# Delta rule heads prepared in two alternating pairs of PSUM banks, in a kernel whose order is written as a plan

## The reference

```python
def even_layer(h, ...):
    p = rms_norm(h, norm_g) @ w_in                       # 2048 x 9232
    qkv_a, z_a, b_a, a_a, glu_b, z_b, q_m, z_m = split(p)
    qkv = silu(causal_depthwise_conv(qkv_a, conv_qkv))   # 4 taps, 3 x 1024 channels
    q, k, v = heads(qkv)                                 # 8 heads of 128
    q = l2_norm(q) * 128 ** -0.5; k = l2_norm(k)
    o = gated_delta_rule(q, k, v, beta, g)               # chunked; needs (I + A)^-1 of each block
    o_a = rms_norm(o, dn_norm_g) * silu(z_a)
    c = causal_depthwise_conv(glu(glu_b), dw_w)          # 31 taps, 1024 channels
    o_b = silu(layer_norm(c)) * silu(z_b)
    o_m = memory_attend(q_m, z_m, ...)
    return concat([o_a, o_b, o_m]) @ w_out
def odd_layer(h, ...):                                   # stick-breaking attention, 16 heads, and memory_attend
```

## Time and profile before

| | |
|---|---|
| median of 3 runs | 1391.09 us (1390.8 to 1392.14) |
| profiled execution | 1390.43 us, of which the span of the core 1388.7 us |
| TensorE busy | 1360.9 us (98%) |
| VectorE busy | 885.6 us (64%) |
| ScalarE busy | 752.8 us (54%) |
| GpSimd busy | 110.5 us (8%) |
| granted TensorE clock, mean | 0.993 |

### The profile page before, as it was taken

The page is one execution under the profiler, slowest core; times in us unless marked ns, Lnnn a source line. Parts: engine busy times, 40 slices in busy tenths (PEclk is TensorE's granted clock), DMA queues, the critical chain, the costliest instruction groups (busy, mean ns, idle before and its releaser), DMA issues.

```text
span 1388.7 us, 17340 instructions
## 1 busy us (share of the span) xinstructions
PE 1360.9 (98%) x6459; PEld 1130.3 (81%) x6459; DVE 885.6 (64%) x1327; ACT 752.8 (54%) x1163; POOL 110.5 (8%) x112
## 2 busy tenths in 40 slices
PE   6999998999989999999999999999999999999998
PEld 5888877888878887888888888888888888888887
DVE  4547698787787898774566544564655645556563
ACT  4545543455524565666444555755756757665341
POOL 1001201010300100000000120020020110000000
PEclk9999999999999999999999999999999999999999
DMA  8565445555554575465365655464564564653652
GB/s 268 194 200 167 154 130 161 150 165 158 146 175 136 186 270 188 130 218 176 123 192 164 212 172 181 140 201 163 177 201 141 177 187 149 191 174 121 195 185 76
DMA packets 134205, 239.27 MB, mean 172 GB/s; under 512 B 13888, under 2 KB 19433, under 8 KB 134121
## 3 DMA queue, kind: packets, MB, share of 16 engines
q1 hardware_dynamic: 131945, 233.96, 53.1%
q10 hardware_dynamic: 2176, 4.19, 0.9%
HBM read 234.32 MB, written 3.80 MB: 171 GB/s over the span
## 4 chain that ended last, share of the span: by engine, by line
PE 93%; DVE 3%; issue 1%; SPq 1%; ACT 1%; DMA 0%; DVEq 0%; ACTq 0%
PE job L1581 27%; PE job L1583 27%; PE job L1582 27%; PE mixer L1601 4%; DVE wlo L1218 1%; PE mixer L1810 1%; PE mixer L1830 1%; PE mixer L1702 1%; DVE reg L1292 1%; PE mixer L1848 1%; PE mixer L1716 0%; PE mixer L1861 0%; PE mixer L1714 0%; DMA raw<-in_ev_w_in_dram 0%; SPq L708 0%
## 5 line engine op out<-in xcount | busy, mean ns | idle before, releaser
L1581 PE MATMUL job<-whi,xhi 128*128 128x512 f32 x1728 | 695.2, 402 | 0.0
L1218 DVE TENSOR_TENSOR wlo<-raw,whi 128x1024 fp32r<-128x1024 f32 x432 | 529.4, 1243 | 239.3 <-ACT whi L890 236.6
L1583 PE MATMUL job<-whi,xlo 128*128 128x512 f32 x1728 | 676.8, 392 | 0.0
L1582 PE MATMUL job<-wlo,xhi 128*128 128x512 f32 x1728 | 675.5, 391 | 0.0
L890 ACT ACTIVATE whi<-raw 128x1024 fp32r<-128x1024 f32 x432 | 445.4, 1056 | 142.3 <-PE job L1583 133.6
L1583 PEld LDWEIGHTS job<-whi,xlo 128*128 128x128 f32 x1728 | 325.7, 189 | 70.9
L1582 PEld LDWEIGHTS job<-wlo,xhi 128*128 128x128 f32 x1728 | 326.9, 189 | 63.2
L1581 PEld LDWEIGHTS job<-whi,xhi 128*128 128x128 f32 x1728 | 326.4, 189 | 63.3 <-issue 0.4
L1442 DVE SCALAR_TENSOR_TENSOR cvr<-cvr,vt 128x255 f32<-128x255 f32 (+14 forms) x240 | 103.5, 491 | 0.0
L917 ACT ACTIVATE proj<-job,rstd 128x512 f32<-128x512 f32 x80 | 50.5, 686 | 50.4 <-PE job L1583 43.9
L1234 DVE TENSOR_TENSOR hid<-hid,job 128x512 f32<-128x512 f32 x48 | 30.8, 683 | 50.6 <-PE job L1583 50.6
(11 more groups left out here) (257 smaller groups left out, 882.9 us busy)
## 6 DMA issues: line engine op xcount, KB each, us to landing
raw<-in_od_w_in_dram SPq DMA_DIRECT2D x160, 512.0 KB, 4.5
raw<-in_ev_w_in_dram SPq DMA_DIRECT2D x144, 512.0 KB, 4.0
raw<-in_ev_w_out_dram SPq DMA_DIRECT2D x48, 512.0 KB, 4.6
raw<-in_od_w_out_dram SPq DMA_DIRECT2D x48, 512.0 KB, 4.7
raw<-in_w_mem_kv_dram SPq DMA_DIRECT2D x32, 512.0 KB, 4.3
hid<-in_x_dram SPq DMA_DIRECT2D x4, 512.0 KB, 7.9
reg<-in_mem_dram ACTq DMA_DIRECT2D x4, 512.0 KB, 6.2
hid<-in_x_dram ACTq DMA_DIRECT2D x4, 512.0 KB, 7.7
```

Of the source, the lines that this page charges most:

```text
L1218: vec.tensor_tensor(wlo[:, c % RING, :, :], raw[:, c % RAWS, :, :], whi[:, c % RING, :, :].bitcast(F32), ALU.subtract).then_inc(s_lo, 1)
L1581: mm(out_, xh, hi, start=first, stop=False)
L1582: mm(out_, xh, lo, start=False, stop=False)
L1583: return mm(out_, xl, hi, start=False, stop=last)
```

## The change

Before, every head was transposed into `mixer0` and `mixer1` and turned back through `mixer2`. Now an even head has `mixer0` and `mixer1` and an odd one `mixer2` and `mixer3`, and each is turned back through the second bank of its own pair (`mixer1` or `mixer3`). The outputs `d7(0)` to `d7(3)` go by turns through `mixer2` and `mixer3` (before: `mixer2`).

In the plan a head takes 3.1 chunks (before 3.5), and `dnB(h - 1)` is placed right behind the next head's `dnT` and `dnC`. Steps that follow in the same stream move with it, those of the convolution only in part. No instruction is added or removed.

```diff
-DN_STEP = 3.5
+DN_STEP = 3.1
...
         for h in range(h0, h0 + 4):
-            s += [(("dnT", h), .2), (("dnC", h), 1.2), (("dnS", h), .9), (("dnU", h), DN_STEP - (2.1 if h > h0 else 1.7))]
-            s += [(("dnB", h - 1), .1)] if h > h0 else []
-        s += [("wait", 1), (("dnB", h0 + 3), 1), (("dnV", g), 2), (("dnR", g), 2.5)]
+            s += [(("dnT", h), .2), (("dnC", h), .6)] + ([(("dnB", h - 1), .6)] if h > h0 else [("wait", .6)])
+            s += [(("dnS", h), .9), (("dnU", h), DN_STEP - 2.3)]
+        s += [("wait", .6), (("dnB", h0 + 3), 1), (("dnV", g), 2), (("dnR", g), 2.5)]
...
             if step == "d7":
-                return [1 if i in (5, 7) else 2]
+                return [2 + i % 2 if i < 4 else 1 if i in (5, 7) else 2]
+            if step in ("dnT", "dnB"):
+                return [0, 1, 2, 3][2 * (i % 2) + (step == "dnB"):2 * (i % 2) + 2]
...
-        def dn_source(c):
+        def dn_source(h, c):
 
-            return (M[0][:, S:2 * S], M[0][:, 0:S], M[1][:, 0:S])[c]
+            m = M[2 * (h % 2):2 * (h % 2) + 2]
+            return (m[0][:, S:2 * S], m[0][:, 0:S], m[1][:, 0:S])[c]
```

More of the change, by code:

```diff
@@ L570, in banks @@
             if step == "d7":
-                return [1 if i in (5, 7) else 2]
+                return [2 + i % 2 if i < 4 else 1 if i in (5, 7) else 2]
+            if step in ("dnT", "dnB"):
+                return [0, 1, 2, 3][2 * (i % 2) + (step == "dnB"):2 * (i % 2) + 2]
             if step == "d4y":
                 return [1] if i % 7 == BASE else ([1, 2] if i % 7 < 6 else [2])
-            return {"first": [0], "vec": [3], "ba": [0], "bat": [1], "bas": [2], "dnT": [0, 1], "dnB": [2], "dnR": [1], "dnG": [0, 1],
+            return {"first": [0], "vec": [3], "ba": [0], "bat": [1], "bas": [2], "dnR": [1], "dnG": [0, 1],
                     "d4x": [0],
@@ L983, in do_dnC @@
                     col = V_CONV + 24 * (CONV - 1) + dn_tile(h, c)
-                    ins = act(ykqv[:, h % 4, c, :], dn_source(c), ACT.Copy, scale=vt[:, col:col + 1])
+                    ins = act(ykqv[:, h % 4, c, :], dn_source(h, c), ACT.Copy, scale=vt[:, col:col + 1])
                 ins.then_inc(s_tap, 1)
@@ L989, in do_dnS @@
                 y = ykqv[:, h % 4, :, :]
-                act(M[0][:, :].rearrange("p (c s) -> p c s", c=2), y[:, 0:2, :], ACT.Tanh, scale=0.5)
-                act(M[1][:, 0:S], y[:, 2, :], ACT.Tanh, scale=0.5).then_inc(s_th, 1)
+                act(M[2 * (h % 2)][:, :].rearrange("p (c s) -> p c s", c=2), y[:, 0:2, :], ACT.Tanh, scale=0.5)
+                act(M[2 * (h % 2) + 1][:, 0:S], y[:, 2, :], ACT.Tanh, scale=0.5).then_inc(s_th, 1)
             def do_dnB(h):
@@ L1291, in do_dnC @@
                             ve.wait_ge(s_cv4, n + 1 - 3)
-                        vec.scalar_tensor_tensor(out=y[:, r:], in0=dn_source(c)[:, 0:S - r], scalar=vt[:, col:col + 1],
+                        vec.scalar_tensor_tensor(out=y[:, r:], in0=dn_source(h, c)[:, 0:S - r], scalar=vt[:, col:col + 1],
                                                  in1=y[:, r:], op0=ALU.mult, op1=ALU.add).then_inc(s_cv4, 1)
@@ L1298, in do_dnU @@
                 y = ykqv[:, h % 4, :, :]
-                vec.scalar_tensor_tensor(out=y[:, 0:2, :], in0=M[0][:, :].rearrange("p (c s) -> p c s", c=2), scalar=1.0,
+                vec.scalar_tensor_tensor(out=y[:, 0:2, :], in0=M[2 * (h % 2)][:, :].rearrange("p (c s) -> p c s", c=2), scalar=1.0,
                                          in1=y[:, 0:2, :], op0=ALU.add, op1=ALU.mult).then_inc(s_silu, 1)
-                vec.scalar_tensor_tensor(out=y[:, 2, :], in0=M[1][:, 0:S], scalar=1.0, in1=y[:, 2, :],
+                vec.scalar_tensor_tensor(out=y[:, 2, :], in0=M[2 * (h % 2) + 1][:, 0:S], scalar=1.0, in1=y[:, 2, :],
                                          op0=ALU.add, op1=ALU.mult).then_inc(s_silu, 1)
@@ L1307, in do_dnB @@
                 ve.wait_ge(s_tok, h + 1)
-                vec.tensor_copy(nrm[:, h, :], M[2][:, 384:388]).then_inc(s_nrm, 1)
+                vec.tensor_copy(nrm[:, h, :], M[2 * (h % 2) + 1][:, 384:388]).then_inc(s_nrm, 1)
             def do_dnV(g):
@@ L1663, in do_dnB @@
                 pe.wait_ge(s_sq, h + 1)
+                m = M[2 * (h % 2) + 1]
                 for a in range(4):
-                    ins = mm(M[2][:, 384 + a:385 + a], scr[:, 128 * a:128 * a + 128], ones[:, 0:1], start=True, stop=True)
+                    ins = mm(m[:, 384 + a:385 + a], scr[:, 128 * a:128 * a + 128], ones[:, 0:1], start=True, stop=True)
                 ins.then_inc(s_np, 1)
                 y = ykqv[:, h % 4, :, :]
-                turn(M[2][:, 0:128], y[:, 0, 0:128])
-                turn(M[2][:, 128:256], y[:, 2, 0:128])
-                turn(M[2][:, 256:384], y[:, 2, 128:256]).then_inc(s_back, 1)
+                turn(m[:, 0:128], y[:, 0, 0:128])
+                turn(m[:, 128:256], y[:, 2, 0:128])
+                turn(m[:, 256:384], y[:, 2, 128:256]).then_inc(s_back, 1)
             def do_dnR(g):
```

4 lines of the change are left out of this document (2 added, 2 removed).

## The result

The changed kernel takes **1405.8 us** (median of 4 runs, 1405.18 to 1406.91), the kernel before 1390.94 us beside it (1390.3 to 1392.14): a ratio of 1.0109, interval 1.0094 to 1.0124, so 1.1% slower. The profiled execution took 1405.3 us, its span 1403.6 us, 14.9 us more than the span before.

The account below looks back on a forecast made before the run. TensorE, busy 98% of the span, was taken as the bound, so only its waits and clock could change. Terms summed to +9.2 us on 1390.43 (1399.6), plus 0.66 for the median: 1400.3 us, own range 1395 to 1405, stated range 1391.5 to 1407.

Parts of the forecast that it names:

- `dnB0`, less the wait at head 2: Head 0's `dnB0` follows three chunks and waits 2.4 us for its squares; head 2's 0.9 us wait goes: +1.5 us.
- `dnG3`: The gate `za(0)` moves behind `dnG3` on VectorE, so the 0.5 us wait goes: -0.5 us.
- first `d4x`: Behind the first inversion VectorE gets 3.8 us more, TensorE 2.75; the wait grows from 5.3 to 6.4: +1.1 us.
- head 4: Two groups of taps delay head 4's taps 3.0 us; `dnT5` and `dnB4` wait 5.8 us, before 0.6: +5.2 us.
- `d7(2)`, `d7(3)`, `dnB7`: Behind head 4: waits of 1.3 us for head 5's silu, 1.0 for its norms, 1.5 at `dnB7`: +3.8 (1.5 to 5).
- `gT4` and second `d4x`: Second group: a 2.6 us wait for `glu(1)` comes; the second inversion's 3.9 and `gT4`'s 0.2 go: -1.5 (-2.5 to -0.7).
- clock: First inversion's fall stays, the second's goes (-2.6), head 4's wait brings one (2.2): -0.4 us.
- rival 2: More clock falls: waits at head 0 (2.4) and `gT4` (2.6) cost 1.8 to 3.4 us each: 1404 to 1407; chance 0.15.
- higher bound: At `gT4`: ports locked for the masked copy's whole 1.47 us would make the upper bound 0.8 us higher.
- rival 1: Faster: each inversion's extra chunk of cover counts in full, waits shrink and both falls go: 1380 us; chance 0.08.
- rival 3: Head 4 milder: the two groups of taps are absorbed, head 4 waits 2.8 us, no new fall: 1392; chance 0.12.

Follow-up runs that it names:

- convs_away: Changed kernel with two groups of convolution taps (24, 25), ahead of head 4's taps on VectorE, moved 15 chunks later: 1400.23 us (1.0072 to the kernel before).
- b_convs: Kernel before with groups of convolution taps moved out of VectorE's fullest stretches, nothing else: 1385.16 us (0.9953).
- glu_early: Changed kernel with `glu(1)` ahead of `dnG5` instead of behind `dnG7`, nothing else moved: 1400.24 us (1.0062 to the kernel before).
- a_d4x2: Changed kernel with `d4x` and all behind it in its stream two chunks later, inversion and transposes unmoved: 1402.99 us (1.0074 to the kernel before).
- b_d4x2: Kernel before with `d4x` and all behind it in its stream two chunks later, inversion and transposes unmoved: 1391.1 us (1.0000).
- inv_later: Changed kernel with one chunk more between the inversion's steps twice (`INV_STEP` 3.5, 3.2 instead of 2.5, 2.2): 1399.23 us (1.0058 to the kernel before).
- b_convs_glu: Kernel before with the moved groups of taps of `b_convs`, and `glu(1)` two chunks earlier on VectorE and ScalarE: 1383.95 us (0.9949).
- dnB0_later: Changed kernel with `dnB0` one chunk later on all engines, nothing else moved: 1406.28 us (1.0102 to the kernel before).
- step35: Changed kernel with 3.5 chunks for a head again instead of 3.1, all else kept: 1393.71 us (1.0024 to the kernel before).

## Why the prediction was right, and where it was not

The time was forecast at 1400.3 us, within 1391.5 to 1407, slower. It is 1405.8. Its terms against the profile after:

| term | forecast | measured |
|---|---|---|
| `dnB0`, less the wait at head 2 | +1.5 | +1.4 (2.31 - 0.92) |
| `gT0` | none | +1.0 (1.19, was 0.2) |
| `dnG3` | -0.5 | -0.5 |
| first `d4x` | +1.1 | +1.1 (6.39 - 5.33) |
| head 4 | +5.2 | +4.7 (3.20 + 2.06 - 0.6) |
| `d7(2)`, `d7(3)`, `dnB7` | +3.8 | +2.9 (0, 1.15, 1.75) |
| `gT4` and second `d4x` | -1.5 | -0.5 (2.96 - 0.2 + 0.66 - 3.88) |
| clock | -0.4 | +3.1 |
| behind chunk 150 | none | +1.0 (see below) |
| sum | +9.2 | +14.2; the span +14.9 |

The last term is from the lists of waits: 5.1 us for VectorE's `xlo` where before it was 3.3, 0.2 of it in the start-up, and 0.5 for `mix` where it was 1.1. 0.7 us is left over, in small waits that I did not assign.

- **The waits were forecast well**, and by one method: when does TensorE come to a step in the new order, and when is the step's input there by the durations of before. VectorE's path to the transposes grew by 3.8 us (29.2 against 25.5), exactly as counted; head 4's taps began 5.7 us behind `dnT4` (forecast 5.9). `convs_away` shows the two groups of taps as the cause at head 4. `d7(2)` didn't wait: TensorE came to it 33.4 us behind `d5e3` (309.64 - 276.28), where I had 30.8, by the fall of the clock just ahead, which my sum kept as a separate term.
- **The clock was the mis-sized term**, 3.5 us of the 5.7 missed. I let the waits of 5.8 us bring a fall and the waits of 2.4 and 2.6 none (that was rival 2). In the profile the wait of 2.31 us at `dnB0` has one of 3.4 us behind it (1.7 us lost), the wait of 2.96 at `gT4` another (1.4, since part lies in the wait); the first inversion's cost 2.0 and head 4's 2.4. So rival 2 came true beside the forecast. `b_convs` has TensorE's steps in the order of before and neither fall, so it prices them: from chunk 56 to 70 the kernel before takes 60.07 us and `b_convs` 54.41, of which the waits are 5.33 and 1.40, and 1.7 us are left for the first fall; from chunk 110 to 120 it is 46.59 and 40.01 with waits of 3.88 and none, 2.7 us for the second. I had 1.8 and 2.6. The whole low time halved, as the Trainium skill has it (TensorE: Matmul & The Clock Gate, HAM oscillation), would be 3.4 us for each; here the part of a low stretch that lies inside the wait cost nothing.
- **The step that failed at gT0**: the sum has no term for it; what stands ahead of `glu(0)` on VectorE was not looked at. `dnR0` moved from behind it to right ahead of it, so that its small operations (156.94 to 158.6) now stand on VectorE in front of the product of `glu(0)`:

```profile
154.57 2.46 DVE L1221 TENSOR_TENSOR wlo<-raw,whi 128x1024 fp32r<-128x1024 f32 x2 [1.60 <-ACT whi L893]
156.94 0.27 DVE L1339 CAST pick<-ident 128x24 fp32r<-128x24 f32 x1
...
158.64 1.36 DVE L1428 SCALAR_TENSOR_TENSOR proj<-proj 128x1024 f32<-128x1024 f32 x1
```

- **gT4** waited 2.96 us where I took 2.6 of 1.6 to 3.5. The product of `glu(1)` took 2.28 us beside GpSimd's masked copies and 1.22 us without them in `glu_early`, 1.06 us more. The second copy began 1.05 us ahead of the product, and ended 1.2 us into it (370.69 + 2.25 - 371.74):

```profile
370.69 2.25 POOL L832 TENSOR_TENSOR reg<-hid,mix 128x512 f32<-128x512 f32 x1
371.74 2.28 DVE L1428 SCALAR_TENSOR_TENSOR proj<-proj 128x1024 f32<-128x1024 f32 x1
```

By the Trainium skill (SBUF — State Buffer, Who interferes with whom) the operation that starts second is blocked until the other's ends. The trace agrees: the product ended 1.08 us behind the copy, about its time alone. What it loses is the rest of the copy, and not the copy's whole length, which the prediction had taken from that page for its higher bound. The second `d4x` was to lose its wait and kept 0.66.
- **What the prediction did not ask**: whether either half of the change is free. With the new order the banks cost 1 to 1.5 us (1405.8 and 1404.72; spans 1403.6 and 1402.1), which the intervals of the two ratios don't tell from nothing. With the old one they cost 4.3, so their price rests on where `dnB` stands. The wait at `d7(3)`, which the prediction laid on the new banks, is there without them.
- **The rivals**: rival 1 (1380 us) and rival 3 (1392) fell by their own signs, VectorE's path to the transposes and head 4's taps.

The clock's terms in the table are worked out as half the low time behind the wait. At `dnB0` they can be measured too, as the wait of 2.3 us is the same in three kernels: from chunk 26 to chunk 35 `convs_away`, with no low stretch, takes 31.5 us, the changed kernel, with 3.4 us, 33.1, and `a_d4x2`, with 6.8 us, 34.5. So the stretches cost 1.6 and 3.1 us. Open: head 4's, the first inversion's and `gT4`'s share in the changed kernel were not measured in this way, and the 1.0 us behind chunk 150 was not followed up.

## What to carry to other kernels

When a hand-written order is drawn closer, list for each engine what now stands between an input and its user, above all the filler work that another stream keeps at its old place: two groups of taps made 3.0 of the 5.3 us at head 4, and by the rows one norm step made the wait at `gT0`, though no run moved it. A wait moved to a later user of the same late engine is no gain (`b_d4x2`); taking filler off that engine between the two is (`b_convs`), less what the filler costs where it goes. Check the engine named in a list of waits against the row's times: the one that ended last just ahead of the start is the cause. Count every new wait of about 1.8 us or more with a fall of the clock behind it as a possible cost of its own.

## What the runs showed of the hardware

**Waits of about 1.8 to 3 us have a stretch at 1.2 instead of 2.4 GHz behind them in some kernels and not in others.** The same wait of 2.3 us at `dnB0` had a low stretch of 3.4 us behind it in the changed kernel, `glu_early` and `inv_later`, of 6.8 in `a_d4x2`, and none in `convs_away`. The 2.27 us behind chunk 144 of `b_convs` had one of 3.4 us; the same wait of 2.25 us in `b_convs_glu` none. The 1.75 us at `dnB7` had none in the changed kernel, 3.4 us in `inv_later` and 6.8 us in `dnB0_later` and `a_d4x2`. No single wait of 1.4 us or less had one to itself. The first `d4x`, wherever it waited 5.3 us or more, always had one, of 6.8 or 10.2 us. Even the start-up has 3.4 us in some profiled executions and 6.8 in others, about 1 us apart at chunk 10. I found nothing in the traces that tells beforehand which it will be, and no run was made for it.

**So one kernel can have two times.** The ten executions of `step35` fall into 1392.5 to 1394.0 us at a mean granted clock of 0.994 or 0.995, and 1397.0 to 1397.8 us at 0.991. The four of `a_d4x2` go from 1397.4 us (0.994) to 1404.2 us (0.987). A change of order that is worth a few us can be hidden by this, as in `dnB0_later`, which won 4.1 us at its place and lost 4.2 to two stretches of low clock elsewhere.

**In three places here a VectorE operation that began beside GpSimd's masked copy lasted until the rest of the copy was over.** The product of `glu(1)` took 2.28 instead of 1.22 us and ended 1.08 us behind the second copy. The product of `za(1)` took 1.63 instead of 1.22 us and ended 1.08 us behind the first (370.74). In the kernel before, the tap operation that began at 187.97 took 1.52 us where its neighbours took 0.47, and ended 0.3 us behind the copy. The copy is held up too: the second one began inside the product of `za(1)` and took 2.25 us, the first 1.30. Which of the two pays, and how much, would then depend on the start times; no run was made for it.
